# Two-column modulation products between transform tiles, and ScalarE's part in the shift of the outer columns

## The reference, cut to what matters

```python
def ada_params(cond, w, b):
    m = jax.nn.silu(cond) @ w + b
    return jnp.split(m, 3, axis=-1)          # shift, scale, gate
...
    sh_l, sc_l, gt_l = ada_params(c, ada_w[i], ada_b[i])
    sh_c, sc_c, gt_c = ada_params(c_ctx, ada_w[i], ada_b[i])
    hl = rmsnorm(x, norm_g[i]) * (1.0 + sc_l[:, None, :]) + sh_l[:, None, :]
    hc = rmsnorm(ctx, norm_g[i]) * (1.0 + sc_c) + sh_c
    ...
    ol = fourier_mixer(hl, ...)              # layer 0: u, z = h @ w_in; y = fft2(u).real; (y*silu(z)) @ w_out
```

## Time and profile before

| | before |
|---|---|
| median of 3 runs | 946.14 us (945.64 to 947.05) |
| the profiled execution's own time | 945.66 us |
| its span in the profile | 943.9 us |
| TensorE busy | 923.4 us, 98% of the span |
| VectorE busy | 545.6 us, 58% |
| ScalarE busy | 351.0 us, 37% |
| GpSimd busy | 245.4 us, 26% |
| mean granted TensorE clock | 0.997 of full speed |

### The profile page before, as it was taken

The page is one execution under the profiler, slowest core; times in us unless marked ns, Lnnn a source line. Parts: engine busy times, 40 slices in busy tenths (PEclk is TensorE's granted clock), DMA queues, the critical chain, the costliest instruction groups (busy, mean ns, idle before and its releaser), DMA issues.

```text
span 943.9 us, 13110 instructions
## 1 busy us (share of the span) xinstructions
PE 923.4 (98%) x4835; PEld 801.0 (85%) x4835; DVE 545.6 (58%) x813; ACT 351.0 (37%) x598; POOL 245.4 (26%) x243
## 2 busy tenths in 40 slices
PE   5999999999999999999999999999999999999997
PEld 5999998888888888888888888888888888888886
DVE  5897769999974422367444444435435445468333
ACT  8453343233133322345323334424323333354223
POOL 4259941766553000014100220012200221011001
PEclk9999999999999999999999999999999999999998
DMA  9752324655545112212211122102121121102222
GB/s 352 299 218 95 112 90 151 194 181 187 186 172 223 56 58 67 90 45 90 77 59 44 45 90 67 68 1 89 67 67 44 44 68 65 56 11 90 90 90 89
DMA packets 28891, 98.78 MB, mean 105 GB/s; under 512 B 3832, under 2 KB 6040, under 8 KB 28592
## 3 DMA queue, kind: packets, MB, share of 16 engines
q1 hardware_dynamic: 26832, 91.10, 28.4%
q0 software_dynamic: 1744, 6.84, 1.9%
q10 hardware_dynamic: 272, 0.26, 0.1%
HBM read 96.07 MB, written 2.10 MB: 104 GB/s over the span
## 4 chain that ended last, share of the span: by engine, by line
PE 89%; DVE 4%; issue 2%; DMA 2%; ACT 2%; POOL 1%; SPq 0%; POOLq 0%; DVEq 0%
PE banks L1720 29%; PE banks L1721 29%; PE banks L1722 29%; DMA raw<-stream 1%; DVE wreg L1195 1%; DVE hreg L1241 1%; ACT hreg L914 0%; POOL gate L656 0%; DMA gate<-x_rows 0%; DVE gate L1186 0%; DVE gate L1189 0%; DVE dist L1205 0%; PE banks L1847 0%; POOL gate L696 0%; DVE ring L1123 0%
## 5 line engine op out<-in xcount | busy, mean ns | idle before, releaser
L1720 PE MATMUL banks<-hreg,ring 128*128 128x512 f32 (+2 forms) x940 | 332.1, 353 | 1.9 <-DVE ring L1123 0.9
L1721 PE MATMUL banks<-hreg,ring 128*128 128x512 f32 (+2 forms) x940 | 331.3, 352 | 0.0
L1722 PE MATMUL banks<-hreg,ring 128*128 128x512 f32 (+2 forms) x940 | 329.5, 351 | 0.0
L1105 DVE TENSOR_TENSOR ring<-raw,ring 128x512 fp32r<-128x512 f32 x192 | 140.0, 743 | 244.4 <-ACT ring L708 243.1
L708 ACT ACTIVATE ring<-raw 128x512 fp32r<-128x512 f32 x192 | 118.6, 629 | 362.2 <-PE banks L1722 274.2
L1720 PEld LDWEIGHTS banks<-hreg,ring 128*128 128x128 f32 x940 | 177.3, 189 | 27.0 <-issue 3.6
L1722 PEld LDWEIGHTS banks<-hreg,ring 128*128 128x128 f32 x940 | 176.8, 188 | 22.4
L1721 PEld LDWEIGHTS banks<-hreg,ring 128*128 128x128 f32 x940 | 177.4, 189 | 21.1 <-issue 0.2
L623 POOL TENSOR_TENSOR gate<-xreg,gate 128x257 f32<-128x257 f32 (+1 forms) x64 | 74.8, 1198 | 72.7 <-ACT gate L857 56.6
L1137 DVE CUSTOM_DVE_ANT_0 dist<-raw,gate 128x1024 bf16<-128x1024 f32 x64 | 84.5, 1320 | 4.0 <-DMA raw<-stream 0.3
L656 POOL TENSOR_TENSOR gate<-gate 128x512 f32<-128x512 f32 x12 | 17.2, 1429 | 250.7 <-ACT gate L938 249.9
(11 more groups left out here) (229 smaller groups left out, 1094.2 us busy)
## 6 DMA issues: line engine op xcount, KB each, us to landing
raw<-stream SPq DMA_DIRECT2D x148, 512.0 KB, 3.3
gate<-stream SPq DMA_DIRECT2D x10, 512.0 KB, 11.2
gate<-x_rows SPq DMA_DIRECT2D x6, 512.0 KB, 7.0
gate<-x_lat POOLq DMA_DIRECT2D x1, 2048.0 KB, 8.6
xreg<-x_lat POOLq DMA_DIRECT2D x1, 2048.0 KB, 8.2
out<-xreg SPq DMA_DIRECT2D x3, 384.0 KB, 2.6
xreg<-stream SPq DMA_DIRECT2D x2, 512.0 KB, 12.5
gate<-cond_in SPq DMA_DIRECT2D x2, 512.0 KB, 9.9
```

Source lines behind the costliest of these rows:

```text
L1105: dve.tensor_tensor(ring[:, n % 2, 1, c], raw[:, buf, c], f32(ring[:, n % 2, 0, c]), ALU.subtract).then_inc(split_done, 1)
L1720: pe.matmul(out, left[0], right[0], start=start, stop=False)
L1721: pe.matmul(out, left[0], right[1], start=False, stop=False)
L1722: return pe.matmul(out, left[1], right[0], start=False, stop=stop)
```

## The change

The three modulation tiles between the transform's tiles get a moving operand of 2 columns in place of 128; the eight tiles before the transform keep 128. The copy of the outer columns to `dc` goes from VectorE to ScalarE for tiles 0 to 4, ahead of that tile's high parts. For tiles 5 to 7 there is no copy: ScalarE computes the shifted outer columns itself from PSUM (factor `fmul`, bias `base0`), in two ACTIVATEs of one column ahead of the high parts. For these VectorE prepares `base0` in `shift_base`, which stands behind the low parts of tile 3 and the last `early`. VectorE's first shift covers tiles 0 to 4 and its second one tiles 5 to 7, without the three linked instructions that made the shifted values.

```diff
+        base0 = sb("base0", [P, KT, 2])
...
             act.wait_ge(dft_done, k + 1)
             b = 2 * (k % 3)
             src = banks[:, 512 * b:512 * b + 1024].rearrange("p (i n) -> p i n", i=2)
+            if k < DVE_SHIFT:
+                act.activation(dc[:, k, :], src[:, 0, 0:NB + 1:NB], ACT.Copy).then_inc(row_shift, 1)
+            else:
+                act.wait_ge(base_done, 2)
+                for v in range(2):
+                    act.activation(shift0[:, k, v:v + 1], src[:, 0, NB * v:NB * v + 1], ACT.Identity,
+                                   scale=fmul[:, k, v:v + 1],
+                                   bias=base0[:, k, v:v + 1]).then_inc(end_shift, 1)
...
         def transform_lo(k):
-            dve.tensor_copy(dc[:, k, :], src[:, 0, 0:NB + 1:NB]).then_inc(row_shift, 1)
...
+        def shift_base():
+            k = slice(DVE_SHIFT, KT)
+            dve.wait_ge(ada_used, 2 * KT - DVE_SHIFT)
+            add_bias(mod0[:, k, :], pe_columns(7)[:, 0:KT - DVE_SHIFT, :], bias0[:, k], KT - DVE_SHIFT)
+            for v, tokens in ((0, LAT), (1, CTX)):
+                dve.tensor_scalar(base0[:, k, v], mod0[:, k, v], float(np.sqrt(tokens)), None,
+                                  ALU.mult).then_inc(base_done, 1)
+
+        def row_shifts():
+            k = slice(0, DVE_SHIFT)
+            dve.wait_ge(early_dot, 2 * DVE_SHIFT)
+            add_bias(mod0[:, k, :], row_mod[:, :, :], bias0[:, k], DVE_SHIFT)
+            dve.wait_ge(row_shift, DVE_SHIFT)
+            link(dve.tensor_tensor(shift0[:, k, :], dc[:, k, :], fmul[:, k, :], ALU.mult))
+            for v, tokens in ((0, LAT), (1, CTX)):
+                link(dve.scalar_tensor_tensor(...))      # sqrt(tokens) * mod0 + shift0
+
         def add_shift(a, b):
-            dve.wait_ge(row_shift, b)
-            link(dve.tensor_tensor(shift0[:, k, :], dc[:, k, :], fmul[:, k, :], ALU.mult))
-            for v, tokens in ((0, LAT), (1, CTX)):
-                link(dve.scalar_tensor_tensor(...))
             dve.wait_ge(hf_lo, 2 * b)
             link(dve.tensor_copy(hf[0][0][:, k, ends], shift0[:, k, :]))
             dve.tensor_tensor(hf[1][0][:, k, ends], ...).then_inc(shift_done, 1)
...
             if k == 5:
-                dve.wait_ge(early_dot, 2 * DVE_SHIFT)
-                add_bias(mod0[:, 0:DVE_SHIFT, :], row_mod[:, :, :], bias0[:, 0:DVE_SHIFT], DVE_SHIFT)
-                dve.wait_ge(ada_used, 2 * KT - DVE_SHIFT)
-                add_bias(mod0[:, DVE_SHIFT:KT, :], pe_columns(7)[:, 0:KT - DVE_SHIFT, :], ...)
-                add_shift(0, KT // 2)
+                row_shifts()
+                add_shift(0, DVE_SHIFT)
+            if k == KT - DVE_SHIFT:
+                shift_base()
         fold_lo(1)
-        add_shift(KT // 2, KT)
+        dve.wait_ge(end_shift, 2 * (KT - DVE_SHIFT))
+        add_shift(DVE_SHIFT, KT)
...
-            def ada_tile(t, o):
+            def ada_tile(t, o, repeats):
...
-                                     csf[:, k:2 * KT:KT].unsqueeze(1).to_broadcast([P, WARM, 2]),
+                                     csf[:, k:2 * KT:KT].unsqueeze(1).to_broadcast([P, repeats, 2]),
...
-                ada_tile(j, bank(7 - j // 4, 2 * WARM, 2 * WARM * (j % 4)))
+                ada_tile(j, bank(7 - j // 4, 2 * WARM, 2 * WARM * (j % 4)), WARM)
...
-                    ada_tile(KT + 1 + k, bank(7, 2 * WARM, 2 * WARM * k))
+                    ada_tile(KT + 1 + k, bank(7, 2, 2 * WARM * k), 1)
```

More of the change, by code:

```diff
@@ L360, in build @@
         f_scaled = sem("transform_factor")
+        base_done, end_shift = sem("shift_base_done"), sem("later_shift")
         xa_done, pair_done = sem("x_half_scaled"), sem("x_folded")
@@ L1244, in transform_lo @@
                                              op1=ALU.subtract).then_inc(hf_lo, 1)
-            def add_shift(a, b):
-                ends = slice(0, HALF + 1, HALF)
-                k = slice(a, b)
-                dve.wait_ge(row_shift, b)
+            def shift_base():
+                k = slice(DVE_SHIFT, KT)
+                dve.wait_ge(ada_used, 2 * KT - DVE_SHIFT)
+                add_bias(mod0[:, k, :], pe_columns(7)[:, 0:KT - DVE_SHIFT, :], bias0[:, k],
+                         KT - DVE_SHIFT)
+                for v, tokens in ((0, LAT), (1, CTX)):
[6 more added lines that the diff above has]
+                dve.wait_ge(row_shift, DVE_SHIFT)
                 link(dve.tensor_tensor(shift0[:, k, :], dc[:, k, :], fmul[:, k, :], ALU.mult))
@@ L1255, in add_shift @@
                                                   op0=ALU.mult, op1=ALU.add))
+            def add_shift(a, b):
+                ends = slice(0, HALF + 1, HALF)
+                k = slice(a, b)
                 dve.wait_ge(hf_lo, 2 * b)
@@ L1268, in _ @@
                 if k == 5:
-                    dve.wait_ge(early_dot, 2 * DVE_SHIFT)
-                    add_bias(mod0[:, 0:DVE_SHIFT, :], row_mod[:, :, :], bias0[:, 0:DVE_SHIFT], DVE_SHIFT)
-                    dve.wait_ge(ada_used, 2 * KT - DVE_SHIFT)
-                    add_bias(mod0[:, DVE_SHIFT:KT, :], pe_columns(7)[:, 0:KT - DVE_SHIFT, :],
-                             bias0[:, DVE_SHIFT:KT], KT - DVE_SHIFT)
-                    add_shift(0, KT // 2)
+                    row_shifts()
+                    add_shift(0, DVE_SHIFT)
+                if k == KT - DVE_SHIFT:
+                    shift_base()
             fold_lo(1)
-            add_shift(KT // 2, KT)
+            dve.wait_ge(end_shift, 2 * (KT - DVE_SHIFT))
+            add_shift(DVE_SHIFT, KT)
             dve.wait_ge(feat_hi, 1)
```

## The result

| | before | changed |
|---|---|---|
| median | 946.60 us (6 runs) | 949.46 us (6 runs, 945.37 to 951.53) |
| ratio to before | | 1.0032, 95% interval 1.0021 to 1.0043 |
| the profiled execution | 945.66 us, span 943.9 | 945.37 us, span 943.5 |
| granted clock of single executions | 0.997 in the profiled one | 0.996 in the profiled one, 0.990 to 0.992 in the five others |

The changed kernel is slower by 0.3%. The forecast was 945.1, no measurable change; the time lies above its range (944.2 to 947.3). The profiled execution is the fastest of the six, so its trace shows less of the loss than the median holds.

A forecast was written before the change was run, and what follows sets the result against it. TensorE, busy 98%, was taken as the bound, with 1.3 us of stalls behind VectorE to gain. With the cast first, shift_base's delay included, 1.0 us came off the 946.14 median: 945.1, range 944.2 to 947.3.

The forecast's parts named there:

- rival 2: Narrow tiles between the transform's drop TensorE to 1.2 GHz; 1.3 or 3.8 us lost; chance 0.05 above 1.9 us, shared.
- unseen wait: A wait nowhere located that costs more than 1.9 us; chance 0.05, shared with the clock.
- one slow tile: One transform tile at 1.2 GHz: up to 2.56 us longer, 1.3 us net; chance 0.05, shared with other small losses.
- The cover of 1.3 us: TensorE's stalls behind VectorE, 1.05 us before 59.37 and 0.25 us before 61.85, taken off a slow tile's cost.
- Part 1: Three narrow modulation tiles: weight loading is what costs, 1.76 us a tile, so only 0 to 0.03 us saved.
- Part 2: Copies on ScalarE for tiles 0 to 4: 0.17 us each, bounds 0.07 and 0.27, delays covered by later waits.
- Part 3: shift_base ahead of tile 4's low parts: +0.29 us on VectorE, TensorE's tile 7 0.32 us later.
- Part 4: VectorE's list from tile 4 on: cast first gives -1.0 us, memset first +0.1 us.
- the tie: VectorE's cast at 54.62 and GpSimd's memset at 54.61, 0.01 us apart; whichever starts first decides; leaned to the cast.
- rival 1: GpSimd's memset starts before VectorE's cast and shuts it out: +0.1 us, 946.2; chance 0.35.
- the two orders of cast and memset: Near 54.6 us, cast first gives -1.0 us (945.1), memset first +0.1 us (946.2).
- two slow tiles: Two transform tiles at TensorE's 1.2 GHz: 3.8 us lost, 950 us.

The follow-up runs named there:

- e2: The kernel before with only the three modulation tiles between the transform's narrowed to 2 columns: 948.87 us, ratio 1.0035 to the kernel before.
- e4: The changed kernel run once more, nothing altered, for its scatter and a second trace: 948.01 us, ratio 1.0020 to the kernel before.
- e8: The changed kernel with 2 columns only in the first of the three tiles, 128 in the other two: 945.29 us, ratio 0.9991 to the kernel before.
- e9: The changed kernel with the eight tiles before the transform at 2 columns too: 960.42 us, ratio 1.0149 to the kernel before.
- e10: The changed kernel with 2 columns only in the third of the three tiles, 128 in the other two: 945.83 us, ratio 0.9998 to the kernel before.
- e1: The changed kernel with 128 columns again in the three tiles, all moved work kept: 944.36 us, ratio 0.9984 to the kernel before.
- e7: The changed kernel with 128 columns in the three tiles, shift_base before the last early, fold_sum(2) before GpSimd's wait, memsets behind its two DMAs: 944.52 us, ratio 0.9983.
- e3: The changed kernel with 64 columns in the three tiles: 944.33 us, ratio 0.9985 to the kernel before.
- e5: The changed kernel with 128 columns in the three tiles and shift_base behind tile 4's low parts: 944.91 us, ratio 0.9986 to the kernel before.
- e6: The kernel before with GpSimd's fold_sum(2) moved ahead of its wait for the transform's end and the memsets: 944.92 us, ratio 0.9989.

## Why the prediction was wrong, point by point

**The step that failed is the weighing of rival 2, the clock.** The sum put the clock's cost at nothing, and a loss above 1.9 us, by the clock or by an unseen wait, got a chance of 0.05; one slow tile shared another 0.05 with other small losses. A loss above 1.9 us is what happened: the changed kernel's median is 2.9 us over the one before. The mechanism of the rival was described rightly: narrow tiles between the transform's, a fall to 1.2 GHz, slower transform tiles. What I set against it was one stretch, the one-column token sum of 1.75 us at a clock of 1.00. In all twelve traces here that token sum kept its level, while seven of the twelve narrow tiles between the transform's that began at the full level were followed by a slow stretch (the traces of the changed kernel, e2, e4, e8, e9 and e10), the single one of e8 among them. So the row was a true observation, and what failed is carrying it over from one place of the kernel to another: the token sum lies alone in a long run of dense products, and the change makes three such bursts, 2.6 us of transform apart, in a stretch that begins with the modulation tiles. Which of the differences matters is not shown. And I had left unasked what the 64-fold repetition in the kernel before was doing, though my own sum said that it cost nothing: e9 shows that without it TensorE stays at half pace up to the transform and into it. The prediction also read its clock column too far: the clock "seen at 0.50 only at the very end" left out the start of the kernel, where the first records are slow and the column reads 1.00 (e9).

**Its price was of the right size.** The prediction had 1.3 us for one slow tile and 3.8 (950) for two; the median is 949.46. The terms are off: a slow stretch of 3.5 us cost 5.92 - 4.36 = 1.56 us and not up to 2.56, and in the traces the stretches are 3.3 to 9.6 us long and up to 13 us in sum (e4). The cover of 1.3 us that the prediction took off came out in the profiled execution: `project_u(0)` 1.69 late, kind 0 only 0.29 (62.14 against 61.85). Between e1 and the changed kernel, where there is no such cover, lie 0.36% (by e4) to 0.48% (by the result above), 3.4 to 4.5 us.

**Part 1, the columns' own cost: right.** 1.75 us for a narrow tile at full clock, against 1.76. The part's conclusion "nothing" was wrong only through the clock: it is the term that should have held the 3.4 to 4.5 us.

**Part 2, ScalarE: right in effect, sizes off both ways.** The copy is 0.07 us in spacing, not 0.17, at the lower bound. The two one-column instructions take 0.49 together, not 0.34. Both are covered, and no table load appears.

**Part 3, `shift_base`: right.** 0.34 us between 50.14 and 50.48, low parts at 50.48 against 50.51, `project_u(0)` at 54.29 against 54.38. e7 shows the 0.26 us given back once it is hidden.

**Part 4, the tie: the outcome came true, by luck.** The cast ran in 0.17 us in all traces of the changed family, and the gain of e1 is 1.13 us at kind 0 (forecast 1.0) and 1.7 us in the medians (0.7 to 2.4 by the interval). But the reason I leaned on, that the memset would be the later of the two, failed: in e1 the memset is recorded at 54.52 and the cast at 54.59, the order of rival 1, and still the cast was not shut out. e3 and e10 show the same, and e5 with the second memset, 0.06 to 0.07 us apart. It looks as if GpSimd's hold begins later than its record; the prediction had no such term.

**The range.** It was built on the two orders of cast and memset and on the runs' scatter. The clock case was given no part of it; its own price for two slow tiles, 950, lay outside.

## What to carry to other kernels

An operand that is wider than its result needs may be there for TensorE's clock. Before narrowing it, ask what the same instructions and those behind them would cost at half clock, ask of any row that is said to speak against it whether it lies in the same surroundings, and let the range reach there; columns that hide behind the weight load save nothing by going. A gain made in the same change can be real and be lost in such a fall, so undo the parts one at a time: here the moved work was worth -0.16% and the narrow tiles +0.4%.

## What the runs showed of the hardware that was not expected

- Narrow products (2 columns) were 0.21 to 0.23 us a record apart from 8.6 us on, with TensorE at its lower level, against 0.11 at full level, and 128 records of them, from 8.59 to 36.45 us, did not bring it to the full one (e9). The same records with 128 columns did, within the first 32 (8.60 to 14.63 us) of the kernel before.
- 64 columns kept the clock as well as 128 did, over 11 executions (e3).
- A profile's granted clock can read 1.00 through 40 us at half pace when no change precedes it in the trace (e9).
- A cast of VectorE that is recorded 0.06 to 0.07 us behind the start of a GpSimd memset was not held up (0.17 us; e1, e3, e5, e10); 0.34 and 0.48 us behind it was (0.79 us before, 0.65 in e6).
- What held the clock in the token sum at 406 us, with one column and in all twelve traces, and let it fall behind a single narrow tile at 32.5 us in some executions, stays open.
